# Attention scores in a hybrid decoder layer: the low-half product of k on 64 rows per head, issued ahead of the transposes

## The reference, cut to what matters

```python
# q: (B, nb, 128, 2 kv heads, 8 heads each, 64); kb: previous and own block of 128 keys
scores = einsum('bnqhgd,bnkhd->bnhgqk', qb, kb) * (64 ** -0.5)
scores = where(in_window, scores + bias, NEG_INF)
m      = maximum(max(scores), sink)
p      = exp(scores - m);  probs = p / (sum(p) + exp(sink - m))
out    = einsum('bnhgqk,bnkhd->bnqhgd', probs, vb)
```

## Time and profile before

| | |
|---|---|
| median of 3 runs | 915.75 us |
| the profiled execution | 917.0 us, span 915.3 us |
| busy, share of the span | PE 99%, PEld (weight loads) 83%, DVE 68%, ACT 54%, POOL 54% |
| granted TensorE clock | 0.999 |
| DMA | 120.39 MB, mean 132 GB/s |
| scores (L910) | 256 matmuls |
| transposes (L920) | 128 matmuls |

### The profile page before, as it was taken

The page is one execution under the profiler, slowest core; times in us unless marked ns, Lnnn a source line. Parts: engine busy times, 40 slices in busy tenths (PEclk is TensorE's granted clock), DMA queues, the critical chain, the costliest instruction groups (busy, mean ns, idle before and its releaser), DMA issues.

```text
span 915.3 us, 12593 instructions
## 1 busy us (share of the span) xinstructions
PE 904.0 (99%) x4376; PEld 759.3 (83%) x4376; DVE 625.3 (68%) x1071; ACT 495.3 (54%) x942; POOL 492.3 (54%) x385
## 2 busy tenths in 40 slices
PE   8999999999999999999999999999999999999997
PEld 6888888888888888888888888888878888888885
DVE  5644488664646565656565678678679878989967
ACT  6544345666757575656675664334342534534563
POOL 1156224868686959686868675544562252042237
PEclk9999999999999999999999999999999999999999
DMA  8841975322323235322222243533288550335004
GB/s 274 226 146 41 284 251 160 117 93 81 93 81 93 80 95 160 92 81 82 93 82 89 85 138 104 183 116 115 70 311 309 184 207 1 138 109 213 1 1 183
DMA packets 109646, 120.39 MB, mean 132 GB/s; under 512 B 6528, under 2 KB 79248, under 8 KB 109328
## 3 DMA queue, kind: packets, MB, share of 16 engines
q1 hardware_dynamic: 109584, 119.60, 39.9%
HBM read 87.57 MB, written 35.15 MB: 134 GB/s over the span
## 4 chain that ended last, share of the span: by engine, by line
PE 95%; POOL 2%; DVE 1%; issue 1%; ACT 1%; DMA 0%; DVEq 0%; POOLq 0%; ACTq 0%
PE acc L893 50%; PE acc L1066 11%; PE acc L768 9%; PE ps_m L1066 6%; PE ps_t L1066 6%; PE ps_t L910 3%; PE ps_m L940 3%; PE acc L836 2%; PE ps_t L920 2%; PE ps_t L775 1%; PE ps_t L789 1%; PE ps_m L789 1%; DMA x_both<-in_x 0%; POOL rstd_o L1610 0%; POOL w_b L1619 0%
## 5 line engine op out<-in xcount | busy, mean ns | idle before, releaser
L893 PE MATMUL acc<-mv,w_hi 128*128 128x512 f32 x1344 | 352.9, 392 | 0.8 <-ACT c L1236 0.8
L893 PEld LDWEIGHTS acc<-mv,w_hi 128*128 128x128 f32 x1344 | 244.9, 188 | 46.0 <-issue 1.2
L893 PE MATMUL acc<-mv,w_lo 128*128 128x512 f32 x672 | 181.0, 391 | 0.0
L893 PEld LDWEIGHTS acc<-mv,w_lo 128*128 128x128 f32 x672 | 126.2, 188 | 27.9
L1591 POOL TENSOR_TENSOR w_lo<-sums,w_hi 128x1024 fp32r<-128x1024 f32 x48 | 117.1, 2440 | 48.3 <-ACT w_hi L1184 39.3
L1591 POOL TENSOR_TENSOR w_lo<-raw,w_hi 128x1024 fp32r<-128x1024 f32 (+1 forms) x48 | 93.9, 1957 | 42.7 <-ACT w_hi L1177 33.6
L1066 PE MATMUL acc<-right,left 128*128 128x512 f32 x432 | 98.8, 389 | 0.0
L1066 PEld LDWEIGHTS acc<-right,left 128*128 128x128 f32 x432 | 81.0, 188 | 17.3 <-DVE right L1926 0.5
L1636 POOL TENSOR_SCALAR_AFFINE_SELECT pt_prev<-pt_pack 128x512 fp32r<-128x512 f32 x64 | 41.7, 652 | 84.4 <-DVE pt_pack L1868 84.4
L1386 ACT ACTIVATE prob<-neg_s,neg_max 128x129 f32<-128x129 f32 x128 | 50.6, 397 | 67.4 <-DVE neg_max L1877 67.1
L768 PE MATMUL acc<-mv 128*128 128x512 f32 x288 | 70.0, 394 | 1.0 <-DVE mv L1723 0.6
(11 more groups left out here) (249 smaller groups left out, 1671.3 us busy)
## 6 DMA issues: line engine op xcount, KB each, us to landing
raw<-in_w_in SPq DMA_DIRECT2D x56, 512.0 KB, 4.4
x_both<-in_x SPq DMA_DIRECT2D x8, 512.0 KB, 4.6
ht_d<-sums SPq DMA_DIRECT2D x8, 512.0 KB, 6.6
mix_d<-mix_b SPq DMA_DIRECT2D x8, 512.0 KB, 3.0
ga_d<-gate SPq DMA_DIRECT2D x16, 256.0 KB, 2.0
tb<-tb_d SPq DMA_DIRECT2D x4, 1024.0 KB, 5.1
ub<-mix_d SPq DMA_DIRECT2D x7, 512.0 KB, 3.4
gb_d<-ub SPq DMA_DIRECT2D x7, 512.0 KB, 2.6
```

Source lines behind the costliest of these rows:

```text
L893: ins = nc.tensor.matmul(bank, (w_lo if y == 2 else w_hi)[:, left + k * P:left + (k + 1) * P], right[:, (OPW if y == 1 else 0) + k * HALF: ...
```

## The change

The scores' PSUM region moves by 256 columns, so that head 0's 256 columns end one bank and head 1's begin the next; the transposes' region moves into the rest of that second bank. The low-half product now takes, for each head, the 64 rows that hold q's high part alone (rows 0 to 63 for head 0, 64 to 127 for head 1), so q_lo k_lo is left out of the sum. The two full products come first, then the two 64-row ones. In attend, the scores now come before the transposes; each of the two waits for the other's last read.

```diff
-        ps_s, ps_p = ps_t[:, 0:512], ps_t[:, 512:768]
+
+        ps_s, ps_p = ps_t[:, 256:768], ps_t[:, 768:1024]
...
                 if s:
                     pe.wait_ge(scores_used, s)
+                    pe.wait_ge(ptl_ok, max(s - 3, 8 * p))
                 lo = P if blk == 0 else 0
                 kc = (blk - 1) * P
                 for h in range(2):
-                    for kbuf, a in ((k_hi, True), (k_lo, False)):
-                        ins = nc.tensor.matmul(ps_s[:, h * 256 + lo:(h + 1) * 256], q_st[h][:, blk * P:(blk + 1) * P],
-                                               kbuf[:, kc + lo:kc + 256], start=a, stop=not a, skip_group_check=True)
+                    nc.tensor.matmul(ps_s[:, h * 256 + lo:(h + 1) * 256], q_st[h][:, blk * P:(blk + 1) * P],
+                                     k_hi[:, kc + lo:kc + 256], start=True, stop=False, skip_group_check=True)
+                for h in range(2):
+                    rows = slice(h * HEAD_DIM, (h + 1) * HEAD_DIM)
+                    ins = nc.tensor.matmul(ps_s[:, h * 256 + lo:(h + 1) * 256], q_st[h][rows, blk * P:(blk + 1) * P],
+                                           k_lo[rows, kc + lo:kc + 256], start=False, stop=True, skip_group_check=True)
                 ins.then_inc(scores_ok, 1)
...
                 if s:
                     pe.wait_ge(ptl_ok, s)
+                pe.wait_ge(scores_used, 8 * p + min(blk + 3, 8))
...
                 if 5 <= k < 13:
                     values(p, k - 5)
+                if k < 8:
+                    scores(p, k)
                 if 3 <= k < 11:
                     transpose_p(p, k - 3)
-                if k < 8:
-                    scores(p, k)
```

## The result

The changed kernel takes 935.3 us (median of 4, 934.73 to 936.51) against 915.75: ratio 1.0214 (95% interval 1.0202 to 1.0226), **slower by 19.6 us**. Forecast were 914.2 us and a range of 911.5 to 924.0. The profiled execution takes 934.73 us with a span of 933.0, 17.7 more than that of before.

What follows compares the result with a forecast made beforehand. TensorE (PE), busy 99% of the span, was taken as the bound. The 64-row pair's -7.5 us and the waits' +5.9 us gave -1.6 us, carried to the median as 914.2 us, range 911.5 to 924.0.

Steps and rivals of the forecast that it cites:

- What bounds the kernel: TensorE (PE), busy 99% of the span: a microsecond taken from it or a wait added counts in full.
- Part 1, the pair: Scores' two 64-row matmuls load and multiply together, costing one pitch: 7.5 us saved over 64 blocks.
- Part 1, the price of the switch: Changing PE between 128 and 64 rows and back around the scores' pair was taken as free, like the transposes.
- the array running empty: Rival: array empties at 128/64-row changes, 0.16 us each; one exposed per step +7.3 us, both +16.3; chance 0.20.
- Part 2, neutral on PE: Scores before transposes in attend: same instructions, 0.69 us together, added waits cost nothing on PE alone.
- Part 2, the wait at k = 5: Scores of attention step k = 5 wait 0.73 us for DVE's read of block 4, eight times: +5.9 us.
- The wait does not come: Rival: the delay at k = 3 is taken up in the chain, likely gate_mul; -7.5 us stays, 908.2 us; chance 0.08.
- The sum: Whole kernel: -7.5 + 5.9 = -1.6 us, 914.2 us, called no difference, leaning faster.

Runs made afterwards that it cites:

- five_full: Changed kernel with ten matmuls of 256 columns per step on all 128 rows in place of the scores' loops (timing only): 962.44 us.
- one_of_pair: Changed kernel with head 1's low product left out, so one 64-row matmul stands alone: 935.01 us.
- one_narrow: Changed kernel with head 0's low product on 64 rows and head 1's on 128, two switches and no pair: 942.31 us.
- order_only: The change without the 64 rows: high and low product per head on 128 rows, with the change's banks, order and waits: 921.12 us, ratio 1.0048.
- four_changes: Changed kernel with each head's 64-row low product right behind its own 128-row high product, four switches a step: 964.43 us.
- order_gate_early: The change's order, banks and waits on 128 rows, with DVE's gate_mul(n - 1, 1) before its attend of k = 3: 916.51 us, ratio 1.0002.

## Why the prediction was wrong

One row of the kernel before bears on the step that failed, the weight loads of the transposes at k = 3, whose matmuls start at 369.21:

```profile
368.98 0.37 PEld L920 LDWEIGHTS ps_t<-ident,prob 128*128 128x128 f32 x2
```

- **What bounds the kernel**: right. What PE's steps gained in length appeared in the time: their sum grew by 17.6 us in the changed kernel and the span by 17.7, in five_full by 45.5 and 45.2.
- **Part 1, the pair**: right that it takes one pitch (one_of_pair, one_narrow: 0.12 us saved per step).
- **Part 1, the price of the switch**: this step failed. "I take the first: the pair together, changes free" put 0 where two switches cost 0.39 us per step (order_only to one_narrow), about 24 us over 64 steps, of which the pair gives some 9 back. The nearest row was no neighbour: the transposes use all 128 x 128 of the array, and before the change their loads ran ahead like any other's, 0.23 us before the matmul, so their being free said nothing of a change of rows. The bound from the other side, the array running empty, was in the prediction at 0.16 us per switch, and with both switches gave +16.3 us; the profiled execution shows +17.7. That it came so near is in part luck, since its terms were off both ways: 20.5 for the switches, -7.5 for the pair and +3.3 for the waits, where about 24, -9 and +2.5 were measured. I gave that rival 0.20, mostly at half its price, and so left the result outside the range. Its price lacked 0.03 us per switch. The trace shows besides the emptying that the load can't run ahead; how the 0.19 us divide between the two, no run separates.
- The rule of the Trainium skill (TensorEngine Tiling (Array Packing), Key Properties), that a change of tiling mode drains TensorE, agrees with the trace: 0.21 us from the start of the last full matmul to the pair's loads, where its columns need 0.12. So does its other half, that tiles load and multiply in parallel: two loads in 0.19 us, two matmuls in 0.39.
- **Part 2, neutral on PE**: right (order_only, 0.94 us per step without transposes, and 1.16 against 1.15 with them; added waits cost nothing).
- **Part 2, the wait at k = 5**: right in place and chain. For the order alone 4.9 us were forecast and 4.6 measured; in the changed kernel it is 2.5 us by spans and not 5.9, since PE comes later by the switches, as the rival's sum had it (3.3).
- **"The wait does not come"**: false for the change, but what it pointed at, gate_mul and its slow form, was where the wait could be removed.
- **The sum**: -1.6 forecast. Measured +17.7 on the profiled execution: 15.2 for the switches net of pairing, 2.5 for the waits. The term of the waits was itself rounded up (0.73 x 8 is 5.8). The forecast was called no difference, although the prediction's own chances put more on slower (0.44) than on that (0.32).

## What to carry to other kernels

Before packing products on half the array's rows, count the pairs between two switches, not the pairs: here a switch each way cost 0.39 us and a 256-column pair saved 0.12, so one pair lost, two lost, five won, and the break-even works out at between three and four. Where the trace holds no instance of a resource's change, a row that merely resembles it is no price; the bound that assumes the worst keeps a real chance. When one engine's work is reordered, follow who takes its data first: here a delay of 0.48 us, two steps ahead of the bottleneck's next wait, cost 4.6 us over eight head pairs, and moving one DVE operation that is no part of the attention into idle time gave it back.

## What the runs showed of the hardware that was not expected

Two 64-row matmuls of different rows started together, with their loads (0.19 us for two, as for one), and the second was free: the step is 1.21 us with either one or two. A switch between 64 and 128 rows cost 0.19 us either way (four_changes), the same behind 512-column and 256-column matmuls, once per switch and never within a run of 64-row pairs. DVE's scalar_tensor_tensor of 128 x 512 in gate_mul took 1.60 us beside POOL's work, and 0.69 us away from it. It isn't every operation of that size: c_22, with one of its inputs in PSUM, took 0.69 us in order_gate_early (374.02 to 374.71) inside a POOL tensor_tensor of 1.30 us that began at 373.51.
